# Turning the probability tiles of a windowed attention with VectorE blocks and a DRAM round trip

## The reference

```
scores = einsum('bnqchd,bnkchd->bnchqk', qb, kb) * hd ** -0.5
scores = where(valid, scores, -inf)
m = max(scores, axis=-1);  e = exp(scores - m);  den = sum(e, axis=-1)
o = einsum('bnchqk,bnkchd->bnqchd', e, vb) / den
```

## Time and profile before

| | us |
|---|---|
| median of three runs | 1344.05 |
| span of the profiled execution | 1342.2 |
| PE busy | 1331.9 (99%) |
| DVE busy | 781.2 (58%) |
| ACT busy | 507.8 (38%) |
| POOL busy | 531.0 (40%) |

### The profile page before, as it was taken

The page is one execution under the profiler, slowest core; times in us unless marked ns, Lnnn a source line. Parts: engine busy times, 40 slices in busy tenths (PEclk is TensorE's granted clock), DMA queues, the critical chain, the costliest instruction groups (busy, mean ns, idle before and its releaser), DMA issues.

```text
span 1342.2 us, 17647 instructions
## 1 busy us (share of the span) xinstructions
PE 1331.9 (99%) x6262; PEld 1104.3 (82%) x6262; DVE 781.2 (58%) x1253; ACT 507.8 (38%) x1282; POOL 531.0 (40%) x500
## 2 busy tenths in 40 slices
PE   9999999999999999999999999999999999999998
PEld 6887888888888888888888888888888888888887
DVE  6799887842779666565665752148512566134323
ACT  7455646542434444344443688311200011223100
POOL 6975424404458334041340632342067317044020
PEclk9999999999999999999999999999999999999999
DMA  6232312322203032120320332376279644122111
GB/s 240 79 102 87 109 56 79 110 100 72 75 12 84 24 92 64 31 83 22 97 58 30 114 98 88 100 237 220 94 275 412 198 126 157 55 79 63 40 47 47
DMA packets 84823, 139.51 MB, mean 104 GB/s; under 512 B 10464, under 2 KB 41472, under 8 KB 84736
## 3 DMA queue, kind: packets, MB, share of 16 engines
q10 hardware_dynamic: 40288, 75.82, 16.0%
q1 hardware_dynamic: 44448, 62.56, 15.6%
HBM read 108.84 MB, written 29.51 MB: 103 GB/s over the span
## 4 chain that ended last, share of the span: by engine, by line
PE 92%; DVE 5%; issue 1%; ACT 1%; DMA 0%; POOL 0%; SPq 0%; POOLq 0%; DVEq 0%; ACTq 0%
PE bank L1275 28%; PE bank L1280 28%; PE bank L1279 28%; PE bank L1432 2%; PE bank L1412 2%; PE bank L1399 1%; PE bank L1421 1%; DVE xc L1012 1%; PE bank L1525 1%; PE bank L1320 0%; DMA gain_mix<-in_gain_mix 0%; ACT L750 0%; DVE ibuf L1039 0%; DVE qkr L1116 0%; DVE ibuf L1028 0%
## 5 line engine op out<-in xcount | busy, mean ns | idle before, releaser
L549 POOL TENSOR_TENSOR ring<-raw,ring 128x512 fp32r<-128x512 f32 x221 | 310.5, 1405 | 727.1 <-PE bank L1280 642.8
L1275 PE MATMUL bank<-hn,ring 128*128 128x512 f32 x640 | 251.8, 393 | 1.4 <-DVE sgbuf L1000 1.2
L1280 PE MATMUL bank<-hn,ring 128*128 128x512 f32 x640 | 249.4, 390 | 0.0
L1279 PE MATMUL bank<-hn,ring 128*128 128x512 f32 x640 | 249.2, 389 | 0.0
L1275 PE MATMUL bank<-ring,hn 128*128 128x512 f32 x576 | 232.6, 404 | 0.2 <-POOL ring L549 0.2
L1280 PE MATMUL bank<-ring,hn 128*128 128x512 f32 x576 | 225.8, 392 | 0.0
L1279 PE MATMUL bank<-ring,hn 128*128 128x512 f32 x576 | 225.2, 391 | 0.0
L553 POOL TENSOR_SCALAR ring<-raw 128x512 fp32r<-128x512 f32 x221 | 183.5, 830 | 7.9 <-DMA raw<-in_w_rnn_s 7.8
L1275 PEld LDWEIGHTS bank<-hn,ring 128*128 128x128 f32 x640 | 120.2, 188 | 26.7 <-DVE sgbuf L1000 1.6
L1280 PEld LDWEIGHTS bank<-hn,ring 128*128 128x128 f32 x640 | 120.1, 188 | 25.3
L1279 PEld LDWEIGHTS bank<-hn,ring 128*128 128x128 f32 x640 | 120.3, 188 | 24.0
(11 more groups left out here) (181 smaller groups left out, 2153.7 us busy)
## 6 DMA issues: line engine op xcount, KB each, us to landing
raw<-in_w_tail_s SPq DMA_DIRECT2D x104, 256.0 KB, 2.7
g_in<-gate_dram ACTq DMA_DIRECT2D x48, 256.0 KB, 4.4
raw<-in_w_rnn_s SPq DMA_DIRECT2D x45, 256.0 KB, 2.6
raw<-in_w_qkv_s SPq DMA_DIRECT2D x48, 192.0 KB, 2.5
gate_dram<-g_out ACTq DMA_DIRECT2D x32, 256.0 KB, 2.1
raw<-in_w_qkv_s SPq DMA_DIRECT2D x48, 128.0 KB, 2.2
o_dram<-o_buf ACTq DMA_DIRECT2D x48, 128.0 KB, 1.8
o_in<-o_dram ACTq DMA_DIRECT2D x12, 512.0 KB, 3.5
```

Source lines behind the costliest of these rows:

```text
L549: nc.gpsimd.tensor_tensor(ring[:, ring_slot(p), 1], raw[:, p % RAW], ring[:, ring_slot(p), 0].bitcast(F32), ALU.subtract).then_inc(w_ready, 1)
L1275: ins = T.matmul(out, lhs[0], rhs[0], start=first, stop=False)
L1279: T.matmul(out, lhs[0], rhs[1], start=False, stop=False)
L1280: return T.matmul(out, lhs[1], rhs[0], start=False, stop=last)
```

## The change

The transposition on PE and the copy on ACT go away. In their place DVE transposes `scores` in place in squares of 32x32 (one instruction for a tile), and SP puts the squares where they belong: four transfers per tile write them to a DRAM tensor `turn_dram`, and when these have landed, a fifth reads them back as a transposed tile into `probsT`. DRAM has four places for this. The value product of a tile moves one step later, to step A-7.

Since SP is now in that chain, its weight loads can no longer be issued as soon as a slot of `raw` is free. They get fixed places in SP's list, given by `loaded_after(G)`, and on GpSimd the remainder of piece p-1 is now made ahead of the waits for piece p. DVE waits for the four writes (`et_out`) before it puts new scores into the same place.

```
+def loaded_after(G):
+    if G < SLOTS_Q:
+        c, s = divmod(G, NT)
+        return FIRST_QKV + KD * (c + 1) + (KD // 2 if s < 2 else KD)
+    return FIRST_TAIL + max(KD, G - SLOTS_Q + 11)
-LAG_T, LAG_QK, LAG_ET, LAG_PV = 2, 4, 5, 6
+LAG_T, LAG_QK, LAG_ET, LAG_PV = 2, 4, 5, 7
...
+            def turn_probs(g):
+                r = g % 2
+                b0 = 0 if has_prev(g // (HEADS * NT), g % NT) else QUADS
+                squares = turn_dram[g % 4, b0:]
+                sp.wait_ge(et_done, g + 1)
+                if g >= 4:
+                    sp.wait_ge(probsT_in[r], 16 * ((g - 4) // 2 + 1))
+                for i in range(QUADS):
+                    sp.dma_start(squares[:, :, i].rearrange("b i j -> i b j"),
+                                 scores[i * QUAD:(i + 1) * QUAD, r, b0 * QUAD:].rearrange("p (b j) -> p b j", j=QUAD)
+                                 ).then_inc(et_out[r], 16)
+                sp.wait_ge(et_out[r], 16 * QUADS * (g // 2 + 1))
+                if g >= 2:
+                    sp.wait_ge(pv_done, g - 1)
+                sp.dma_start(probsT[:, r, b0 * QUAD:].rearrange("p (b q) -> p b q", q=P),
+                             squares.rearrange("(b c) i a j -> (c i) b (a j)", c=QUADS)).then_inc(probsT_in[r], 16)
+
+            loaded = load_pieces(RAW, FIRST_QKV + KD)
+            for what, G in MAIN_ORDER:
+                if what == "slot":
+                    loaded = load_pieces(loaded, loaded_after(G))
+                elif 0 <= G - LAG_ET < TILES:
+                    turn_probs(G - LAG_ET)
+                if (what, G) == ("step", TILES - 1 + LAG_ET):
+                    break
+            load_pieces(loaded, PIECES)
...
             for p in range(PIECES):
+                if p >= 1:
+                    lo_part(p - 1)
                 if p in PERM_PIECE:
                     permute_hn(PERM_PIECE[p])
                 pool.wait_ge(raw_in[p % RAW], raw_count(p))
...
-                if p >= 1:
-                    lo_part(p - 1)
...
-                    nc.scalar.activation(probsT[:, g % 2, c0:], bank[6][:, c0:2 * P], ACT.Copy).then_inc(etc_done, 1)
...
+                g = A - LAG_ET
+                if 0 <= g < TILES:
+                    c0 = 0 if has_prev(g // (HEADS * NT), g % NT) else P
+                    dve.wait_ge(exp_done, g + 1)
+                    V.transpose(scores[:, g % 2, c0:], scores[:, g % 2, c0:]).then_inc(et_done, 1)
...
-                        dve.wait_ge(et_done, g - 1)
+                        dve.wait_ge(et_out[g % 2], 16 * QUADS * (g // 2))
...
-                    for b in ((0, 1) if has_prev(grp, tile) else (1,)):
-                        ins = T.transpose(bank[6][:, b * P:(b + 1) * P], scores[:, g % 2, b * P:(b + 1) * P], ident[:])
-                    ins.then_inc(et_done, 1)
...
-                    pe.wait_ge(etc_done, g + 1)
+                    pe.wait_ge(probsT_in[g % 2], 16 * (g // 2 + 1))
```

More of the change, by code:

```diff
@@ L35 @@
 CLASSES = (1, 4, 8)
+QUAD = 32
+QUADS = P // QUAD
 OFF_Z_RNN = RNN
@@ L341, in build_layer @@
         gate_dram = nc.dram_tensor("gate_dram", (2 * KD, P, S), F32, kind="Internal").ap()
+        turn_dram = nc.dram_tensor("turn_dram", (4, 2 * QUADS, QUAD, QUADS, QUAD), F32, kind="Internal").ap()
         stat_dram = nc.dram_tensor("stat_dram", (2, TILES, P), F32, kind="Internal").ap()
@@ L402, in build_layer @@
         et_done = sem("et_done")
-        etc_done = sem("etc_done")
+        et_out = [sem("et_out0"), sem("et_out1")]
+        probsT_in = [sem("probsT_in0"), sem("probsT_in1")]
         pv_done = sem("pv_done")
@@ L502, in _, with load_pieces @@
             sp.dma_start(spare_first[:, :, 0], chunk_bias(0).rearrange("p (q i) -> p q i", q=4)).then_inc(bq_in[0], 16)
[L504 to L514, removed]
+            def load_pieces(first, end):
+                for p in range(first, end):
+                    sp.wait_ge(w_ready, p + 1 - RAW)
+                    if p < FIRST_QKV:
+                        load(p % RAW, a["w_rnn_s"][p])
+                    elif p < FIRST_TAIL:
+                        c, k = divmod(p - FIRST_QKV, KD)
+                        for u, col, width, dst in chunk_sources(c):
+                            sp.dma_start(raw[:, p % RAW, dst:dst + width], a["w_qkv_s"][u * KD + k, :, col:col + width]
+                                         ).then_inc(raw_in[p % RAW], 16)
+                    else:
+                        load(p % RAW, a["w_tail_s"][p - FIRST_TAIL])
+                return max(first, end)
```

## The result

The changed kernel takes 1361.76 us (median of four runs, 1360.28 to 1363.31), the kernel before 1344.39 us on the same chip: a ratio of 1.0129, 95% interval 1.0115 to 1.0144. It is 17.4 us slower, where 8.5 us faster were predicted, and it lies outside the range. The profiled execution of it has a span of 1358.5 us.

A forecast was written before the change was run, and what follows sets the result against it. PE was taken to bound the kernel (busy 1331.9 of 1342.2 us). Saving 15.4, less 6.3 for the late load and 0.6 for DVE, gave 8.5 us: median 1335.6 us, range 1327 to 1343 us.

The forecast's parts named there:

- late load: Slot 28: pieces 32 to 35 load late, delaying the rearrangement's second half; PE waits 6.3 us once (4.5 to 10).
- DVE beside GpSimd: First rearrangement, 21 us: four added DVE transpositions exceed the cover, so PE waits 0.6 us (0 to 3.8).
- the far end: PE's 1.5 us wait for ACT's copy in the removed group: counted as 0, with 1.5 us as the most saved.
- The saving on PE: 140 transpositions leave PE; by pitch, 0.22 us per two-block and 0.11 us per one-block tile, 15.4 us in all.
- 4.3 against 5.2 us. SP keeps up: SP's loop of 3.8 us plus 0.5 us of weight issues per step fits in a step of 5.2 us.
- The loop and the landing: SP's round trip per tile: loop 3.8 us, last write landing 2.3 us after its issue (4.6 as bound).
- rival B: SP's loop sets the step through slow 128 B writes: landing 4.0 us, 35 us more, 1371 us; 14%.
- hidden, with 1.7 us to spare: DVE's mask of the tile after next needs the writes landed: 3.5 us against a step of 5.2 us.
- doesn't wait: PE's value product: the read lands 6.4 us after its step's start, wanted at 10.4 us, so no wait.
- Rival C: DVE becomes late: a transposition takes 1.2 us beside GpSimd, giving 1342 us, no measurable change; 11%.
- DVE is free at 417.37, +0.3: Chain to the late load: tile 13's transposition on DVE starts 0.3 us after its step begins on PE at 417.09.
- its 0.33 us: SP's issue time for one weight load, 0.33 us; 16 per chunk make 5.3 us, 0.5 us a step.

The follow-up runs named there:

- the fastest kernel: Changed kernel with loads one piece a slot, rearrangement ahead of piece 32, three places for scores, two PSUM banks for value products: 1335.58 us.

## Why the prediction was wrong

Taken away one after the other, the causes give (us): 1361.8, late load 8.4, bursts 9.4, the single place for value products 7.8, third place 0.6, DVE beside GpSimd 8.6, and 1327.0 is left. That is 2 us under 1344.4 - 15.4 = 1329.0; PE's wait of 1.5 us for ACT's copy, which the prediction kept as the far end, may be a part of it. These are differences between one run and the next, so they add up in any case, and the order sets the sizes: on the changed kernel itself the third place is worth 7.4 and the second place for value products 6.4 us, and DVE, with 32.5 us of work in those 42 us, is no bound in it. Spread loads with the rearrangement in its old place were not tried.

- **The saving on PE, right.** 15.4 us from the pitch is what the products cost. But it was credited to the end in full. In the kernel before, with ACT's copies left in, it brought 7.4 us alone, since at several places DVE and ACT were just in time for the slower PE.
- **SP, the step that failed.** "4.3 against 5.2 us. SP keeps up" holds as a mean. The prediction spread the 16 issues of a chunk over its steps, where the diff has them in two lists of eight: `KD // 2 if s < 2 else KD`. One list is 3.8 us of issue at 0.47 us each, 5.1 us in the one at 504.76, in a single step; 3.6 + 3.8 = 7.4 us against 5.2. Spreading the lists gave back 9.4 us. The loop and the landing in that sum were right (3.6 and 1.8 us), and rival B's price per small packet did not show: the rival was right in its engine and wrong in its mechanism. The waits that followed, of DVE for the writes and of PE for masks and reads, were put at nothing in the prediction.
- **The masks, "hidden, with 1.7 us to spare", failed with it.** In the step of the burst near 510 us the writes come 5 us late, and the slack is 1.7.
- **The value product, "doesn't wait", failed.** The read was counted, and lands in time where no burst is (0.2 us of waits at the end). The other wait on the same line, for `ot_done`, was not looked at. It stands in the order of instructions shown ahead of the prediction, `[waits ot_done,probsT_in0]`, and no row of before had a wait at it. It cost 7.8 us, as measured with spread loads.
- **DVE beside GpSimd, mis-sized.** 0.6 us (0 to 3.8) was predicted, 2.5 us measured with the transpositions alone in the kernel before. In the changed kernel DVE's 20.4 us of work in the first stretch didn't come about: it was busy for 16.5 of 21 us, since PE and the writes held it up. Only the fastest kernel has it, 20.5 us, and there the rearrangement costs 8.6 us in all, with DVE at 20.76 of 21 us behind 404 us too, where the prediction had stopped counting. Rival C's mechanism, a transposition of 1.2 us, is wrong: it stays at 0.43 us.
- **The late load, right in place and kind,** 8.4 us for 6.3. The rearrangement started 1.8 us later against PE than counted: "DVE is free at 417.37, +0.3" left out its wait for the exponential, and the issues came slower (above). In the trace PE waits 4.6 us there, and the lower clock behind it takes 0.11 and 0.31 of two stretches of 4 us, 1.7 us; the last 2 us of the 8.4 weren't located.

## What to carry to other kernels

When waits and bulk transfers share one queue, lay out what stands between two round trips in the order of the program: a mean over steps hides a list of eight, and spreading the same loads gave back 9.4 us. Before an instruction is taken off the engine that bounds, read all the waits of the next instruction, and ask of each producer how late it was for the old, slower pace; here a second PSUM place, which the transposition's bank left free, was worth 7.8 us. A stretch in which another engine is 90% busy, as DVE was here, can become a bound as soon as the waits that hid it are gone.

## What the runs showed of the hardware

**The clock behind a wait.** Products of 512 columns start 0.23 us apart. Behind three waits of PE of 1.4 to 1.5 us each, the next seven start 0.42 to 0.59 us apart, most of them 0.43, and the granted clock of the stretch is below 1.00: the lower level, 1.2 GHz, for some 3.4 us. Two stretches of the changed kernel, behind the waits of slot 28; before, both were at 1.00:

```profile
452.00:456.00 4.00, 1.61 (x5) 1.04 (x6) 3.97 (x8) 1.91 (x10) 3.13 (x3) 0.89 0.20 35
456.00:460.00 4.00, 4.00 (x18) 3.24 (x16) 1.88 (x5) 1.37 (x7) 0.00 (x0) 0.69 0.22 52
```

These seven products cost 1.5 us more than at full clock, as much as one of the waits ahead of them.

**Which DVE work GpSimd slows.** In the kernel with spread loads, three places and two banks, the first row beside GpSimd's split (line 592), the others beside the rearrangement:

```profile
405.42 1.49 DVE L1156 TENSOR_TENSOR qkr<-qkn,cossin 128x256 f32<-128x256 f32 x1
...
412.90 1.26 DVE L1156 TENSOR_TENSOR qkr<-qkn,cossin 128x256 f32<-128x256 f32 x1
...
417.14 0.43 DVE L1117 STREAM_TRANSPOSE scores<-scores 128x256 f32<-128x256 f32 x1
417.50 0.38 DVE L1125 CUSTOM_DVE_ANT_0 scores<-bank,masks 128x256 f32<-128x256 f32 x1
```

The product of two SBUF operands takes three times its 0.42 us beside the rearrangement and more beside the split, while the transposition and the masking from PSUM keep theirs. Why isn't settled by these runs.

**Issues on SP.** The four writes of a tile mostly take 1.8 to 1.9 us to issue, 0.43 us each as a median, and weight loads in a list 0.47 us each. An issue that stands alone takes 0.33 us, one right behind another 0.43 us. That held before, too: of the 144 loads below, 71 were the second half of a piece or came as close, with a median of 0.43 us, and the other 73 took 0.33. Single issues took up to 1.8 us; why isn't shown. Transfers by tile, of before and of after (ns min/median/max):

```profile
L511 SPq DMA_DIRECT2D raw<-in_w_qkv_s x144: 327/330/1510, 169.4 to 691.4; - x144
```

```profile
L525 SPq DMA_DIRECT2D raw<-in_w_qkv_s x144: 327/432/1794, 165.6 to 684.6; - x144
```

The prediction took its 0.33 us from loads that each stood alone; in a list of eight it was low by a third.
